# A gate/up strip's fourth weight sum: from VectorE to GpSimd

## The reference

```python
def swiglu(h, w_gate, w_up, w_down):
    return (jax.nn.silu(h @ w_gate) * (h @ w_up)) @ w_down
...
D_FF = -(-8 * D_MODEL // (3 * 256)) * 256
...
        h = rmsnorm(x, g[4])
        x = x + rmsnorm(swiglu(h, ffn_w_gate[layer], ffn_w_up[layer], ffn_w_down[layer]), g[5])
```

## Time and profile before

| what | value |
|---|---|
| device time, median of 3 runs | 2820.19 us (2819.52 to 2821.58) |
| span of the profiled execution, first to last instruction | 2819.1 us (1.1 us under the median) |
| PE busy | 2805.5 us |
| DVE busy | 2385.6 us |
| ACT busy | 1683.7 us |
| POOL busy | 57.9 us |

### The profile page before, as it was taken

One profiled execution on the slowest core, in us unless ns is written; L12 is line 12 of the kernel. 1 busy time (PEld: TensorE's weight loads), 2 busy tenths in 40 slices (PEclk: granted clock), 3 DMA queues, 4 the chain that ended last, 5 costly groups with the idle time before them and its releaser, 6 DMA issues. The chain is left out here.

```text
span 2819.1 us, 31970 instructions
## 1 busy us (share of the span) xinstructions
PE 2805.5 (100%) x12912; PEld 2331.8 (83%) x12912; DVE 2385.6 (85%) x1570; ACT 1683.7 (60%) x1461; POOL 57.9 (2%) x112
## 2 busy tenths in 40 slices
PE   9999999999999999999999999999999999999998
PEld 8888888888888888888888888778888888888887
DVE  7988787799599988989888777899599889889987
ACT  6666555556366656657565765556456566556654
POOL 0000000000000000000000000000000000000000
PEclk9999999999999999999999999999999999999999
DMA  7674755656556456446648554656555565465654
GB/s 269 238 279 166 274 194 191 239 209 240 193 209 224 177 196 239 177 182 231 216 182 293 186 194 168 236 181 234 215 210 196 191 239 197 170 230 198 235 194 149
DMA packets 274690, 595.13 MB, mean 211 GB/s; under 512 B 9024, under 2 KB 9056, under 8 KB 269168
## 3 DMA queue, kind: packets, MB, share of 16 engines
q1 hardware_dynamic: 267968, 532.72, 53.0%
q0 software_dynamic: 5696, 49.88, 4.5%
q10 hardware_dynamic: 880, 10.49, 1.0%
HBM read 572.08 MB, written 20.97 MB: 210 GB/s over the span
## 5 line engine op out<-in xcount | busy, mean ns | idle before, releaser
L1326 DVE TENSOR_TENSOR w_lo<-wide,w_hi 128x2048 fp32r<-128x2048 f32 x574 | 1299.5, 2289 | 259.1 <-ACT w_hi L667 256.5
L667 ACT ACTIVATE w_hi<-wide 128x2048 fp32r<-128x2048 f32 x574 | 1094.0, 1916 | 510.8 <-PE ps L2189 361.8
L2189 PE MATMUL ps<-w_hi,act_hi 128*128 128x512 f32 x3096 | 822.7, 390 | 0.7 <-ACT w_hi L686 0.5
L2189 PE MATMUL ps<-w_lo,act_hi 128*128 128x512 f32 x3092 | 818.2, 389 | 0.5 <-DVE w_lo L1326 0.5
L2189 PE MATMUL ps<-w_hi,act_lo 128*128 128x512 f32 x3092 | 817.6, 389 | 0.0
L2189 PEld LDWEIGHTS ps<-w_lo,act_hi 128*128 128x128 f32 x3092 | 580.1, 188 | 122.3 <-DVE w_lo L1326 1.9
L2189 PEld LDWEIGHTS ps<-w_hi,act_lo 128*128 128x128 f32 x3092 | 580.3, 188 | 120.9
L2189 PEld LDWEIGHTS ps<-w_hi,act_hi 128*128 128x128 f32 x3096 | 578.7, 188 | 120.4 <-issue 2.1
L1330 DVE TENSOR_TENSOR wide<-wide,wide 128x2048 f32<-128x2048 f32 x141 | 323.0, 2291 | 6.5
L667 ACT ACTIVATE w_hi<-w_sum 128x2048 fp32r<-128x2048 f32 x47 | 90.3, 1921 | 116.9 <-DVE w_sum L1330 101.0
L1330 DVE TENSOR_TENSOR w_sum<-wide,wide 128x2048 f32<-128x2048 f32 x47 | 107.6, 2290 | 37.4 <-PE ps L2189 37.4
(11 more groups left out here) (306 smaller groups left out, 1881.9 us busy)
## 6 DMA issues: line engine op xcount, KB each, us to landing
wide<-in_ffn_w_gate SPq DMA_DIRECT2D x88, 1024.0 KB, 8.1
wide<-in_ffn_w_up SPq DMA_DIRECT2D x88, 1024.0 KB, 7.4
wide<-in_ffn_w_down SPq DMA_DIRECT2D x88, 1024.0 KB, 7.2
wide<-in_odd_w_in SPq DMA_DIRECT2D x48, 1024.0 KB, 5.3
wide<-in_xattn_wv SPq DMA_DIRECT2D x32, 1024.0 KB, 7.0
wide<-in_even_w_in SPq DMA_DIRECT2D x32, 1024.0 KB, 7.3
wide<-in_xattn_wq SPq DMA_DIRECT2D x32, 1024.0 KB, 6.4
wide<-in_xattn_wo SPq DMA_DIRECT2D x32, 1024.0 KB, 6.5
```

The costliest lines, as they stand in the source:

```text
L667: nc.scalar.activation(w_hi[:, c % W_SLOTS, :], src, ACT.Copy).then_inc(hi_done, 2)
L1326: nc.vector.tensor_tensor(w_lo[:, c % W_SLOTS, :], src, w_hi[:, c % W_SLOTS, :].bitcast(F32), ALU.subtract).then_inc(lo_done, 2)
L2189: return nc.tensor.matmul(dst, lhs, rhs, start=start, stop=stop, skip_group_check=loose)
```

## The change

The fourth sum F6 of each summed gate/up strip is taken off DVE and written on POOL's instruction stream, once for each of the ten summed strips of a layer, 20 in all. The other stages that use the scheme keep all four sums on DVE. POOL's sum waits for F2 (`add_done`) and for the `lo` of chunk c+3 (`lo_done`), because it overwrites `b21`, which that instruction reads. Its end raises a new semaphore `f6_done`; ACT's `hi` of chunk c+6 and SP's load into B11's buffer wait for it instead of `add_done`. The counts of `add_done` are recomputed in `added`, since a gate/up strip now raises it three times and not four.

```diff
+    pool_sums = []
...
+    def added(g, form):
+
+        before = 4 * g - sum(1 for k in pool_sums if k < g)
+        return before + ("S", "F4", "F2", "F6").index(form) + 1
+
+    def f6_count(g):
+
+        return pool_sums.index(g) + 1
...
+            if summed and name[:2] == "gu":
+                pool_sums.append(st.g)
...
-                    slot_free.append((1, 4 * st.g + 4))
+                    slot_free.append((2, f6_count(st.g)) if st.g in pool_sums else (1, added(st.g, "F6")))
...
-                    sp.wait_ge(add_done if summed else lo_done, count)
+                    sp.wait_ge((lo_done, add_done, f6_done)[summed], count)
...
                 spill_x(2 * (3 * l + 2))
+                for st in plan[f"gu{l}"]["strips"][1:]:
+                    b11, b21 = wide[(st.n + B11) % WIDE], wide[(st.n + B21) % WIDE]
+                    pool.wait_ge(add_done, added(st.g, "F2"))
+                    pool.wait_ge(lo_done, 2 * (st.c + 4))
+                    nc.gpsimd.tensor_tensor(b21[:], b11[:], b21[:], ALU.add).then_inc(f6_done, 1)
                 reload_x(f"gu{l}", sums_used(f"down{l}", 1))
...
-                act.wait_ge(add_done, 4 * g + 4)
+                if g in pool_sums:
+                    act.wait_ge(f6_done, f6_count(g))
+                else:
+                    act.wait_ge(add_done, added(g, "F6"))
                 hi(c + 6, wide[(st.n + B21) % WIDE][:])
...
             def rest11(st, before_5=nothing, before_7=nothing, before_9=nothing):
                 c, g = st.c, st.g
                 b11, b12, b22, b21 = (src_of(st.n + k) for k in range(4))
-                dve.wait_ge(add_done, 4 * g + 3)
-                add(b21, b11, b21)
+                if g not in pool_sums:
+                    dve.wait_ge(add_done, added(g, "F2"))
+                    add(b21, b11, b21)
                 lo(c + 4, b12)
```

More of the change, by code:

```diff
@@ L82, in stage @@
             pl["strips"].append(st)
+            if summed and name[:2] == "gu":
+                pool_sums.append(st.g)
             for k in range(8 if sets is None else DOWN_LOADS):
                 if summed and k == B11:
-                    slot_free.append((1, 4 * st.g + 4))
+                    slot_free.append((2, f6_count(st.g)) if st.g in pool_sums else (1, added(st.g, "F6")))
                 elif sets is not None and k == B_LOAD + B11:
-                    slot_free.append((1, 4 * second_group(st).g + 4))
+                    slot_free.append((1, added(second_group(st).g, "F6")))
                 elif sets is not None and k >= B_LOAD:
@@ L317, in build @@
         add_done = sem("add_done")
+        f6_done = sem("f6_done")
         snap = sem("snap")
@@ L701, in lead @@
                 before_1()
-                act.wait_ge(add_done, 4 * st.g + 1)
+                act.wait_ge(add_done, added(st.g, "S"))
                 hi(st.c + 1, w_sum[:, (st.c + 1) % W_SLOTS, :])
                 before_2()
-                act.wait_ge(add_done, 4 * st.g + 3)
+                act.wait_ge(add_done, added(st.g, "F2"))
                 hi(st.c + 2, wide[(st.n + B11) % WIDE][:])
@@ L750, in seven @@
                 nc.scalar.activation(ps[:, b + 1, :], ps[:, b, :], ACT.Copy, scale=-1.0).then_inc(snap, 1)
-                act.wait_ge(add_done, 4 * g + 2)
+                act.wait_ge(add_done, added(g, "F4"))
                 hi(c + 4, wide[(st.n + B12) % WIDE][:])
@@ L1355, in lead @@
                 loaded(st.n + B22)
-                dve.wait_ge(add_done, 4 * g + 1)
+                dve.wait_ge(add_done, added(g, "S"))
                 add(b12, b22, b12)
-                dve.wait_ge(add_done, 4 * g + 2)
+                dve.wait_ge(add_done, added(g, "F4"))
                 add(b11, b12, b11)
@@ L2097, in add_b21 @@
                 def add_b21(st):
-                    dve.wait_ge(add_done, 4 * st.g + 3)
+                    dve.wait_ge(add_done, added(st.g, "F2"))
                     add(src_of(st.n + B21), src_of(st.n + B11), src_of(st.n + B21))
```

## The result

The changed kernel takes 2839.43 us (three runs, 2834.6 to 2840.09) against 2820.19: slower, ratio 1.0063 with an interval of 1.005 to 1.0077. The profiled execution of the changed kernel is the fastest of the three, 2834.6 us, with a span of 2832.9 us, 13.8 us more than before. The other two have a mean granted clock of 0.997 in place of 0.999 and spans of 2837.7 and 2838.3.

The account below looks back on a forecast made before the run. PE was taken as the bound, running matmuls without a gap. DVE's relief 0, 18 regular strips 0, first summed strips 1.12 and 2.04 us: 3.2 us added to the median 2820.19 gave 2823.4 us, range 2818 to 2842.

Parts of the forecast that it names:

- the stated range: Whole kernel: a time from 2818 to 2842 us.
- the slower side that had 0.30: Whole kernel: measurably slower, through lateness in every strip; 0.13 for up to 2842 us, 0.17 for up to 2866.
- the forecast case of no measurable change: Whole kernel: 2823.4 us, own range 2819 to 2826, within 0.2% of no change; chance 0.55.
- lateness in every strip: Gate/up strips: POOL's sum ends too late in each, up to 2842 us for a part, 2866 for more; chance 0.30.
- the sum: Whole program: 0 for DVE, 18 x 0 for regular strips, 1.12 and 2.04 for first summed strips; 3.2 us in all.
- Nothing to gain from DVE's relief: Gate/up stages: removing 20 sums, 45.8 us of DVE time, is worth 0 us because PE hides it.
- POOL's own time, 4.47 us: POOL's F6: at most two 1.96 us passes plus 0.56 us fixed cost; lower bound 1.96 us.
- POOL waits for the DVE instruction ahead and gets into the gap behind the `lo` of c+4, so regular strips cost 0: 18 regular strips: POOL starts at 1060.20, ends at 1064.67, 0.55 us before the limit; cost 0.
- POOL gets in between two DVE instructions with no gap: First summed strips: POOL starts right after the `lo` of c+4; PE waits 1.12 us in gu0, 2.04 in gu1.
- the 7.1 that the prediction had named as a sign of being wrong: Regular strips: POOL has 7.1 us for its sum; lasting longer from its start would show the prediction wrong.
- the rival's: Every summed strip: POOL starts only after the `lo` of c+5, 2.12 us over the limit in 18; 2866 us; chance 0.30.
- The late load is hidden, 3 us are left: Regular strip: load into B11's buffer issued at 1064.7, not 1060.23; chunk c+8 ready 1074.8, needed 1077.81.

Follow-up runs that it names:

- the kernel with the gap: Only the two first summed strips' sums on POOL, DVE's `lo` of c+5 waiting for them, against the kernel before the change: 2822.27 us, ratio 1.0009.

## Why the prediction was right and wrong

The time lies in the stated range and on the slower side that had 0.30, not in the forecast case of no measurable change. That the range holds it is in good part luck: its upper part stood for lateness in every strip, and the 16 strips between cost nothing. The loss came from two first strips, two entries and the clock; the sum had 3.2 us for the first and nothing for the other two.

- *Nothing to gain from DVE's relief*: held. With 16 sums moved and no new wait the time is that of before.
- *POOL's own time, 4.47 us*: held, 4.45 us behind DVE and 4.62 us alone. The Trainium skill's price (GPSIMD Engine Reference, "Elementwise — side-by-side cycle accounting"), 4497 ns, agrees with both within 3%. The reason given, two passes and a fixed cost, was not tested.
- *POOL waits for the DVE instruction ahead and gets into the gap behind the `lo` of c+4, so regular strips cost 0*: held, with 6.51 us per sum and no wait.
- *POOL gets in between two DVE instructions with no gap*: this step failed. It was read from one root of one element at 2147.01 and carried over to a long sum. In the first summed strips the sum waited for the next `lo` as well, 8.71 us in all, over the 7.1 that the prediction had named as a sign of being wrong; PE waited 3.05 and 3.05 us where the prediction had 1.12 and 2.04. With a gap put in, the waits are 0.7 and 0.7. The mechanism there was the rival's, which had put it on every strip; its figures for these strips were 3.32 and 4.24. Most of the way from 2.04 to 0.7 in gu1 is that the trace before had DVE later there: from the start of the `lo` of c+3 to PE's readiness for c+6 it was 11.35 us, and 12.57 in the kernel with the gap (12.43 in the changed kernel). Why is not known. What the root did differently was not settled.
- *The late load is hidden, 3 us are left*: the step failed at the end of the stage. For the chunk that was checked, c+8, it holds; the loads "queued behind it on SP" were waved through. Their delay adds up to 4.9 us at the entries to the down stages: before, the instruction of `right_banks` that PE waits for ended there at 1304.53, and PE began the product that needs it at 1305.42, so there was 0.9 us of cover. The windows in which no PE wait was seen end at 1290 and 2570, ahead of both entries.
- *The clock* was not in the sum. It adds 1.6 us in the profiled run, and by the rounded mean clock 2.8 to 8.5 us more in the two others.

The new waits, 11.0 us, the lower clock, 1.6 us, and the slower first matmuls, about 0.15 us behind each of the four waits (2.87 us for a chunk of 2.72), make 13.2 of the 13.8 us of the profiled span. The rest was not followed.

## What to carry to other kernels

Before work is moved to POOL beside a stream of two-input DVE instructions, look at the stream's gaps: here the sum's time was its own plus the rest of the DVE instruction ahead, plus the next one where that followed without a gap, and then DVE was held in turn. Two in a row is the most that these runs show. A margin must be followed to the end of the stage and through every load that waits for the moved instruction, since the strip in the middle hides what the first and the last do not. On a kernel whose PE never stops, each new wait of a few us can also cost clock.

## What was not expected of the hardware

DVE's stream kept POOL out without a gap and let it in with one of 0.38 us: 8.71 against 6.51 us for the same sum. A held DVE instruction shows no idle time; it shows as 6.22 us of busy time in place of 2.29. And of two PE waits of 3.05 us in one execution, one was followed by half the clock and the other was not.
